# Sums of squares gathered with the residual, centring and scaling in turns, and two interleaved weight slots in a decoder trunk's LayerNorms

## The chip, the cores and the metric

The kernel runs on one core of one Trainium2 chip. The metric is the device time of one execution in microseconds (us), a median over several executions. The core's engines are TensorE (PE: matmuls; PEld is its weight load), VectorE (DVE), ScalarE (ACT), GpSimd (POOL) and SyncE (SP, which here only issues DMAs). Each engine works through its own list of instructions in order and waits on semaphores for the others.

## The reference

Two layers of a decoder trunk are computed for 512 prompt tokens and 8 x 4 sample tokens, 544 columns in all, with a model width of 1024. Each layer has a token mixer (RG-LRU, then gated DeltaNet), a cross-attention into 256 memory tokens, and a channel mixer (dense SwiGLU, then eight experts of which each token takes two). Each of these six sub-layers ends in a post-norm:

```python
def _layer_norm(x, g, b):
    mu = jnp.mean(xf, axis=-1, keepdims=True)
    var = jnp.mean(jnp.square(xf - mu), axis=-1, keepdims=True)
    return ((xf - mu) * lax.rsqrt(var + LN_EPS) * g + b).astype(x.dtype)

x = _layer_norm(DN_ALPHA * x + mix, p['ln_g'][i, 0], p['ln_b'][i, 0])
xa = _mem_attention(x, mem_k[i], mem_v[i], p['xa_wq'][i], p['xa_wo'][i])
x = _layer_norm(DN_ALPHA * x + xa, p['ln_g'][i, 1], p['ln_b'][i, 1])
ff = _swiglu(x, ...) if i % 2 == 0 else _moe_ffn(x, ...)
x = _layer_norm(DN_ALPHA * x + ff, p['ln_g'][i, 2], p['ln_b'][i, 2])
```

## The kernel before

The activations lie feature by feature: `x` has 128 partitions and 8 tiles (`KT`) of 544 columns. A mean over the features is therefore a matmul with a matrix of ones, which leaves the sum in all partitions. The columns are handled in two halves of 272, one PSUM bank each; `pair(i)` is banks 2i and 2i + 1.

**Weights.** A weight slot is a 1024 x 128 block of 512 KB. SP loads the slots in one fixed order into four buffers (`raw`). For the precise projections POOL splits each slot into a high part `wh` and a low part `wl`, of which there are two buffers each; the split of slot s + 2 waits until PE has used slot s (`w_used`). The activations are split too: `xh` and `xl`, or `hh` and `hl`. `lin_tile` then multiplies three groups of 16 matmuls, `wh` by `xh`, `wl` by `xh`, `wh` by `xl`, and signals `w_used` after the last. `linear` runs eight slots on alternating PSUM pairs. Keys and values of the memory (`kv`) take the raw slots as they are.

**The norms.** LN0 and LN1 follow the first layer's mixer and attention, LN2 its SwiGLU, LN3 and LN4 the second layer's mixer and attention. `layer_norm(5)` stands only in a branch for experts that overflow; the usual branch ends in another form of norm. Around a norm the engines do this:

- DVE, `residual`: for each tile that PE finishes, the new `x` (line 1666) and the running sum of the tiles (`add_tile`, L1656). In the SwiGLU (`experts`) the eight running sums come behind the last tile.
- PE, `layer_norm`: the ones-matmul of the sum (L570) into pair 2; then for LN0 to LN2 a part of the second layer's keys and values as filler (`KV1_AT` says which tiles: 4, 8 and 4 in the three norms; L600 for keys, L604 for values); then the ones-matmuls of the eight squares (L577) into pair 3; then the rest of the filler.
- DVE: eight centrings (L1644), and after the scale is known eight scalings (L1647), and eight low parts (L1633).
- ACT: eight squares (L1172) in two alternating buffers `lnsq`, then logarithm and exponential (L1177, L1178) for the inverse root, eight high parts (L1182), eight results (L1186). The copies of the filler's results (L1141 to L1145) stand between the squares and between the results. PE's next projection waits for the last of them (`kv_ev`).

The order is written by hand on each engine. Behind LN0 ACT sends half of the new keys to memory and waits for all outputs so far, since the next copies reuse that buffer:

```python
piece(0, 0)
act.wait_ge(w_used, S_LOUT + 8)
piece(0, 1)
piece(0, 2)
layer_norm(0)
act.dma_start(O["mem_k"][1][:, 0:4, :], A_st).then_inc(out_done, 16)
act.wait_ge(out_done, 80)
attention(0)
```

`piece` loads 2 MB of cached keys and values; it and the outputs of ACT go through ACT's own DMA queue. `attention` begins on PE with the query projection, on ACT with the copies of its eight tiles, one per slot; from its third slot on PE waits for such a copy (`q_ev`). Behind LN2 comes the DeltaNet's projection, which is interleaved with a side projection of `x` itself (L810); behind LN4 comes the router (L1022), which also reads `x`.

## Time and profile before

| | |
|---|---|
| Median of 3 runs | 2652.28 us (2652.21 to 2659.44) |
| The profiled execution's own time | 2667.02 us |
| Its span, first to last instruction | 2665.0 us |
| Mean granted TensorE clock | 0.931 of full speed |
| PE busy | 2407.8 us, 90% of the span |
| DVE busy | 854.4 us, 32% |
| ACT busy | 536.4 us, 20% |
| POOL busy | 961.3 us, 36% |
| Chain of waits: share of PE | 73% |
| Chain of waits: DVE, ACT, POOL | 10%, 3%, 2% |

The first rows say who works, the last two who sets the end: the chain is followed back from the last instruction, at each step to what released it. A timeline row has the start in us from the span's start, the duration in us, engine, line, operation, the tiles written and read, the count, and in brackets the idle time ahead of it with the engine and line that ended it. Rows with a count are several instructions merged.

### The profile page before, as it was taken

What the parts mean: (1) busy time and instruction counts of PE and PEld (TensorE: products, weight loads), DVE (VectorE), ACT (ScalarE), POOL (GpSimd) and SP (SyncE); (2) the same over time, 40 slices, a digit from 0 to 9 for tenths busy, and PEclk for the clock granted to TensorE, in tenths of its full rate; (3) what the DMA queues carried; (4) which work ended last, traced back from release to release, by engine and by line L of the source; (5) the groups of instructions that cost most, each with busy time, mean ns of one, the idle gap of its engine ahead of it and who ended that gap; (6) DMA issues with size and microseconds to landing.
All of it is one profiled execution on the core that took longest, in us unless ns stands there. A gap on an engine that the chain in (4) does not pass through costs nothing.

```text
span 2665.0 us, 42930 instructions
## 1 busy us (share of the span) xinstructions
PE 2407.8 (90%) x17290; PEld 2284.6 (86%) x17290; DVE 854.4 (32%) x1423; ACT 536.4 (20%) x1017; POOL 961.3 (36%) x1397
## 2 busy tenths in 40 slices
PE   8998889999999987999999888889689999999993
PEld 8988858899999967899989777777579999999993
DVE  3673222211011037666666542412301000000004
ACT  2450320310011033333322211321200000100103
POOL 4546614588888725433322103544100000000001
PEclk9999999999999988999988777899789999999996
DMA  7314341322222221211111101341255677788884
GB/s 285 99 61 177 126 182 59 115 88 79 88 87 87 79 71 59 58 59 59 58 52 59 35 25 64 148 160 64 79 188 180 220 238 238 232 266 268 279 286 161
DMA packets 98376, 347.55 MB, mean 130 GB/s; under 512 B 13488, under 2 KB 18736, under 8 KB 93344
## 3 DMA queue, kind: packets, MB, share of 16 engines
q1 hardware_dynamic: 73136, 279.08, 31.2%
q10 hardware_dynamic: 19056, 44.65, 4.7%
q0 software_dynamic: 6016, 21.43, 2.2%
q8 instruction: 122, 2.00, 0.3%
q14 instruction: 46, 0.38, 0.0%
HBM read 318.66 MB, written 26.47 MB: 130 GB/s over the span
## 4 chain that ended last, share of the span: by engine, by line
PE 73%; DVE 10%; issue 7%; DMA 4%; ACT 3%; POOL 2%; ACTq 0%; DVEq 0%; SPq 0%; POOLq 0%
PE ps L548 29%; PE ps L1073 14%; PE ps L1088 8%; PE ps L727 6%; DMA raw<-weights 2%; PE ps L600 2%; PE ps L577 2%; PE ps L604 1%; PE ps L936 1%; PE ps L638 1%; PE ps L932 1%; DVE x L1647 1%; PE ps L915 1%; POOL wl L471 1%; PE ps L774 1%
## 5 line engine op out<-in xcount | busy, mean ns | idle before, releaser
L467 POOL TENSOR_TENSOR wh<-raw,tab 128x256 fp32r<-128x256 f32 x672 | 425.5, 664 | 940.7 <-PE ps L548 744.2
L471 POOL TENSOR_TENSOR wl<-raw,wh 128x256 fp32r<-128x256 f32 x672 | 507.3, 785 | 0.0
L1073 PE MATMUL ps<-work,raw 128*128 128x128 f32 (+6 forms) x3072 | 424.8, 300 | 13.4 <-DMA raw<-weights 11.0
L1073 PEld LDWEIGHTS ps<-work,raw 128*128 128x128 f32 x3072 | 420.5, 191 | 16.3 <-DVE work L2112 6.8
L548 PE MATMUL ps<-xh,wh 128*128 128x272 f32 x2048 | 309.8, 304 | 41.4 <-ACT work L1353 10.6
L548 PEld LDWEIGHTS ps<-xh,wh 128*128 128x128 f32 x2048 | 282.4, 199 | 50.8 <-issue 18.2
L548 PE MATMUL ps<-xh,wl 128*128 128x272 f32 x2048 | 296.8, 295 | 0.0
L548 PE MATMUL ps<-xl,wh 128*128 128x272 f32 x2048 | 281.8, 288 | 1.5 <-DVE xl L1633 1.4
L548 PEld LDWEIGHTS ps<-xh,wl 128*128 128x128 f32 x2048 | 275.3, 193 | 1.8 <-issue 0.5
L548 PEld LDWEIGHTS ps<-xl,wh 128*128 128x128 f32 x2048 | 265.5, 188 | 2.6 <-DVE xl L1633 2.6
L517 POOL DMA_DIRECT2D rows_y<-moe_h x8 | 4.3, 538 | 656.9 <-DVE moe_h L2105 656.9
L1088 PE MATMUL ps<-work,raw 128*128 128x128 f32 (+6 forms) x1536 | 218.0, 298 | 0.8 <-DVE work L2112 0.8
L1088 PEld LDWEIGHTS ps<-work,raw 128*128 128x128 f32 x1536 | 209.6, 190 | 1.6 <-DVE work L2112 1.4
L2112 DVE TENSOR_TENSOR work<-moe_h,ps 128x128 f32<-128x128 f32 (+6 forms) x96 | 30.6, 319 | 440.1 <-ACT moe_h L1563 440.1
L1563 ACT ACTIVATE moe_h<-ps 128x128 f32<-128x128 f32 (+6 forms) x96 | 29.0, 302 | 396.4 <-PE ps L1073 396.3
L1713 DVE TENSOR_TENSOR work<-work,ps 128x544 f32<-128x544 f32 x24 | 17.3, 721 | 225.8 <-PE ps L548 225.8
L2105 DVE COPY moe_h<-ps 128x256 f32<-128x256 f32 (+1 forms) x64 | 25.1, 391 | 197.2 <-PE ps L1061 155.6
L727 PE MATMUL ps<-hh,wh 128*128 128x272 f32 x384 | 81.4, 294 | 6.7 <-DVE hl L1633 6.7
L727 PE MATMUL ps<-hh,wl 128*128 128x272 f32 x384 | 80.4, 292 | 0.0
L727 PE MATMUL ps<-hl,wh 128*128 128x272 f32 x384 | 80.4, 292 | 0.0
L1172 ACT ACTIVATE lnsq<-x 128x544 f32<-128x544 f32 x40 | 26.3, 657 | 210.0 <-DVE x L1644 195.0
L1666 DVE SCALAR_TENSOR_TENSOR x<-x,ps 128x544 f32<-128x544 f32 x32 | 23.1, 721 | 139.9 <-PE ps L548 139.9
(358 smaller groups left out, 3121.3 us busy)
## 6 DMA issues: line engine op xcount, KB each, us to landing
raw<-weights SPq DMA_DIRECT2D x488, 512.0 KB, 3.9
moe_h<-cache SPq DMA_DIRECT2D x6, 2048.0 KB, 8.9
moe_h<-cache ACTq DMA_DIRECT2D x4, 2048.0 KB, 13.6
work<-cache SPq DMA_DIRECT2D x4, 2048.0 KB, 8.9
moe_h<-rows_x POOLq DMA_DIRECT2D x14, 512.0 KB, 7.8
rows_x<-lnsq ACTq DMA_DIRECT2D x9, 512.0 KB, 11.0
work<-scratch ACTq DMA_DIRECT2D x16, 272.0 KB, 4.2
work<-cache ACTq DMA_DIRECT2D x2, 2048.0 KB, 10.4
```

The lines of the kernel that those rows point to most:

```text
L467: nc.gpsimd.tensor_tensor(flat(h1[:, k0:k1]), flat(r1[:, k0:k1]), one_col, MUL).then_inc(pool_hi, 1)
L471: low = nc.gpsimd.tensor_tensor(flat(l1[:, k0:k1]), flat(r1[:, k0:k1]), flat(h1[:, k0:k1]).bitcast(F), SUB)
L548: last = mm(ps[:, 2 * i + h, 0:HT], w[:, par_, k, :], a[:, k, h * HT:(h + 1) * HT], start=(n == 0 and k == 0), stop=(n == 2 and k == KT - 1))
L577: last = mm(ps[:, 6 + h, 0:HT], ones, lnsq[:, k % 2, h * HT:(h + 1) * HT], start=(k == 0), stop=(k == KT - 1))
L600: last = mm(ps[:, b, 0:MEM], raw[:, q, k, :], A_mem[:, k, :], start=(k == 0), stop=(k == KT - 1))
L604: last = mm(ps[:, b, mt * P:(mt + 1) * P], A_mem[:, k, mt * P:(mt + 1) * P], raw[:, q, k, :], start=(k == 0), stop=(k == KT - 1))
L638: last = mm(ps[:, 4 + tt // 2, (tt % 2) * MEM:(tt % 2 + 1) * MEM], A_q[:, 2 * h + kk, tt * P:(tt + 1) * P], A_k[:, 2 * h + kk, :], start=( ...
L727: last = mm(ps[:, 2 * d + h, 0:HT], w[:, s % 2, k, :], a[:, f, h * HT:(h + 1) * HT], start=(f == 0 and m == 0), stop=(f == FT - 1 and m == 2))
L1073: last = mm(ps[:, j // 2, (j % 2) * c:(j % 2 + 1) * c], raw[:, slot % RAW, k, :], M_x[:, r % 2, k, 0:c], start=(k == 0), stop=(k == KT - 1))
L1088: last = mm(ps[:, 2 + d % 2, 0:c], raw[:, slot % RAW, k, :], M_h[:, f, 0:c], start=(f == 0), stop=(f == FT - 1))
L1563: s(A(M_s[:, f % 2, 0:c], ps[:, f % 2, 0:c], ACT.Silu), m_silu, e12 + f + 1)
L2112: s(V.tensor_tensor(M_h[:, f, 0:c], M_s[:, f % 2, 0:c], ps[:, f % 2, c:2 * c], MUL), m_h, e12 + f + 1)
```

## The change

The sums of squares are now formed ahead of the norm, from tiles that are not yet centred. While the last projection runs, ACT squares each new tile (`squares`) and DVE adds it (`add_square`, after `add_tile`). PE then makes two ones-sums, of the tiles and of the squares. ACT squares the mean, DVE subtracts it from the mean of squares, and clamps at zero. The centring, which needs the mean alone, moves behind: DVE centres tile 0 and tile 1 while it waits, then centres and scales by turns. The ones-sums swap their PSUM pairs. In the SwiGLU the running sums move to the tiles of the second half, whose loop is written out.

The filler is cut otherwise: one tile stands ahead of the ones-sums, all others behind; their copies on ACT stand between the high parts. Behind LN0, LN1 and LN3 the first two slots of the next projection are interleaved: both groups with `xh` of slot 0 and slot 1, then both groups with `xl`. ACT issues the cache pieces of LN0 and LN3 behind the norm. In the router's loop the first turns move from k = 3 to k = 5 and wait for LN4's last scaling. The norm of the overflow branch keeps the old form as `last_norm`.

```diff
-KV1_AT = {0: (0, 2, 4), 1: (4, 7, 12), 2: (12, 14, 16)}
+KV1_AT = {0: (0, 4), 1: (4, 12), 2: (12, 16)}
...
             def linear(slot, direct, ah, al, freed, base, fresh=None):
-                for s in range(8):
+                if fresh is not None:
+                    pairs = [lin_steps(slot + s, direct, s, s, ah, al, fresh=fresh, per=2 * KT) for s in range(2)]
+                    for steps in pairs:
+                        next(steps)
+                        next(steps)
+                    for steps in pairs:
+                        for _ in steps:
+                            pass
+                for s in range(0 if fresh is None else 2, 8):
...
             def layer_norm(n):
+                if n in KV1_AT:
+                    lo, hi = KV1_AT[n]
...
+                    kv(1, lo, lo + 1)
+                pe.wait_ge(z_sum, n + 1)
+                for h in range(2):
+                    last = mm(ps[:, 6 + h, 0:HT], ones, lnsq[:, 0, h * HT:(h + 1) * HT], start=True, stop=True)
+                last.then_inc(ln_sum, 1)
+                pe.wait_ge(z_sq, n + 1)
+                for h in range(2):
+                    last = mm(ps[:, 4 + h, 0:HT], ones, lnsq[:, 1, h * HT:(h + 1) * HT], start=True, stop=True)
+                last.then_inc(ln_var, 1)
+                if n in KV1_AT:
+                    kv(1, lo + 1, hi)
+                    pe.wait_ge(kv_ev, 16 + hi)
...
+            def squares(n):
+                act.preload_act_table_set("natural_log_exp_and_others")
+                for t in range(KT):
...
+                    if t >= 2:
+                        act.wait_ge(z_acc, (KT - 2) * n + t - 1)
+                    s(A(lnr[:, :] if t else lnsq[:, 1, :], x[:, t, :], ACT.Square), z_pw, KT * n + t + 1)
...
             def layer_norm(n):
...
+                act.wait_ge(ln_sum, n + 1)
+                s(A(two(lnsq[:, 0, :]), pair(3), ACT.Square, scale=D ** -0.5), z_mean, n + 1)
+                if lo < hi:
+                    kv(1, lo)
+                act.wait_ge(z_var, n + 1)
+                s(A(lnr[:, :], lnr[:, :], ACT.Ln, bias=pc("eps5"), scale=1.0 / D))
+                s(A(lnr[:, :], lnr[:, :], ACT.Exp, scale=-0.5), ln_std, n + 1)
...
+                for k in range(KT):
+                    upper(n, k)
+                    if lo + 1 + k < hi:
+                        kv(1, lo + 1 + k)
+                for k in range(KT):
+                    result(n, k)
...
             piece(0, 0)
+            squares(0)
+            layer_norm(0)
             act.wait_ge(w_used, S_LOUT + 8)
             piece(0, 1)
             piece(0, 2)
-            layer_norm(0)
             act.dma_start(O["mem_k"][1][:, 0:4, :], A_st).then_inc(out_done, 16)
...
             def layer_norm(n):
+                dve.wait_ge(z_mean, n + 1)
+                centre(0)
+                dve.wait_ge(ln_var, n + 1)
+                s(V.tensor_tensor(two(lnr[:, :]), pair(2), two(lnsq[:, 0, :]), SUB))
+                s(V.tensor_scalar(lnr[:, :], lnr[:, :], 0.0, None, ALU.max), z_var, n + 1)
+                centre(1)
+                dve.wait_ge(ln_std, n + 1)
+                for k in range(KT):
+                    if k >= 2:
+                        centre(k)
+                    s(V.tensor_tensor(x[:, k, :], x[:, k, :], lnr[:, :], MUL), ln_n, n * KT + k + 1)
...
+            def add_square(t, n):
+                if t:
+                    dve.wait_ge(z_pw, KT * n + t + 1)
+                    add = V.tensor_tensor(lnsq[:, 1, :], lnsq[:, 1, :], lnr[:, :], ADD)
```

The order of the instructions shows it at three places. On ACT, around LN0, from the first cache piece (`work<-cache`, `moe_h<-cache` are the pieces) to the query copies at the end, the list before was:

```order
L1199 DMA work<-cache 128x2x2048
L1199 DMA moe_h<-cache 128x2x2048 x2
L1167 ACT_TABLE_LOAD
L1172 ACTIVATE lnsq<-x 128x544
L1141 ACTIVATE work<-ps 128x256
...
L1182 ACTIVATE xh<-x,par 128x544 x8
...
L1186 ACTIVATE x<-x,par 128x544 x6
L1329 DMA out_mem_k<-work 128x1024
L1204 ACTIVATE work<-ps 128x544 x8
```

The squares, the filler's copies and the results followed the pieces. On ACT at the same place it is now:

```order
L1265 DMA work<-cache 128x2x2048
L1202 ACT_TABLE_LOAD
L1210 ACTIVATE lnsq<-x 128x544
L1210 ACTIVATE lnr<-x 128x544 x7
L1225 ACTIVATE lnsq<-ps 128x544
...
L1214 ACTIVATE xh<-x,par 128x544 x5
L1219 ACTIVATE x<-x,par 128x544 x8
L1265 DMA moe_h<-cache 128x2x2048 x2
L1396 DMA out_mem_k<-work 128x1024
L1270 ACTIVATE work<-ps 128x544 x8
```

Two of the three pieces moved from ahead of the norm to a place directly ahead of the key output. On PE, around LN1, from the last group of the output projection to the first slots of the SwiGLU, the list before was:

```order
L548 MATMUL ps<-xl,wh 128x272 x16
L570 MATMUL ps<-lnsq,tab 128x272 x2
L600 MATMUL ps<-work,raw 128x256 x24
L577 MATMUL ps<-lnsq,tab 128x272 x16
L600 MATMUL ps<-work,raw 128x256 x8
L604 MATMUL ps<-raw,work 128x128 x64
L548 MATMUL ps<-xh,wh 128x272 x16
L548 MATMUL ps<-xh,wl 128x272 x16
L548 MATMUL ps<-xl,wh 128x272 x16
```

PE now has at this place:

```order
L548 MATMUL ps<-xl,wh 128x272 x16
L624 MATMUL ps<-work,raw 128x256 x8
L586 MATMUL ps<-lnsq,tab 128x272 x2
L590 MATMUL ps<-lnsq,tab 128x272 x2
L624 MATMUL ps<-work,raw 128x256 x24
L628 MATMUL ps<-raw,work 128x128 x64
L548 MATMUL ps<-xh,wh 128x272 x16
L548 MATMUL ps<-xh,wl 128x272 x16
L548 MATMUL ps<-xh,wh 128x272 x16
L548 MATMUL ps<-xh,wl 128x272 x16
L548 MATMUL ps<-xl,wh 128x272 x32
```

Sixteen ones-matmuls became two, one filler tile moved ahead of them, and the two groups with `xl` of slots 0 and 1 moved behind all four groups with `xh`. On DVE, the last tile ahead of LN1 and the norm, before:

```order
L1666 SCALAR_TENSOR_TENSOR x<-x,ps 128x544
L1656 TENSOR_TENSOR lnsq<-lnsq,x 128x544
L1644 SCALAR_TENSOR_TENSOR x<-ps,x 128x544 x8
L1647 TENSOR_TENSOR x<-x,lnr 128x544 x8
L1633 TENSOR_TENSOR xl<-x,xh 128x544 x8
```

DVE now has there, down to the second turn of centring and scaling:

```order
L1762 SCALAR_TENSOR_TENSOR x<-x,ps 128x544
L1745 TENSOR_TENSOR lnsq<-lnsq,x 128x544
L1752 TENSOR_TENSOR lnsq<-lnsq,lnr 128x544
L1714 SCALAR_TENSOR_TENSOR x<-ps,x 128x544
L1719 TENSOR_TENSOR lnr<-ps,lnsq 128x544
L1720 TENSOR_SCALAR lnr<-lnr 128x544
L1714 SCALAR_TENSOR_TENSOR x<-ps,x 128x544
L1726 TENSOR_TENSOR x<-x,lnr 128x544 x2
L1714 SCALAR_TENSOR_TENSOR x<-ps,x 128x544
L1726 TENSOR_TENSOR x<-x,lnr 128x544
```

The sum of squares joined each tile of the projection, and six of the eight centrings moved between the scalings.

## Rows read from the trace of the kernel before

**Rows 1.** Timeline of PE around LN0 (columns as described above).

```profile
261.33 1.19 PE L570 MATMUL ps<-lnsq,tab 128*128 128x272 f32 x4 [1.64 <-DVE lnsq L1656]
...
269.26 8.03 PE L577 MATMUL ps<-lnsq,tab 128*128 128x272 f32 x32
...
291.21 4.00 PE L548 MATMUL ps<-xh,wh 128*128 128x272 f32 x16 [7.01 <-ACT work L1141]
...
305.36 2.16 PE L548 MATMUL ps<-xh,wh 128*128 128x272 f32 x16
```

**Rows 2.** Timelines of DVE (scalings of LN1, then LN0) and ACT (high parts, LN1).

```profile
477.46 6.04 DVE L1647 TENSOR_TENSOR x<-x,lnr 128x544 f32<-128x544 f32 x8 [13.87 <-ACT lnr L1178]
...
278.89 8.75 DVE L1647 TENSOR_TENSOR x<-x,lnr 128x544 f32<-128x544 f32 x8 [10.24 <-ACT lnr L1178]
...
478.29 6.96 ACT L1182 ACTIVATE xh<-x,par 128x544 fp32r<-128x544 f32 x8 [0.93 <-DVE x L1647]
```

**Rows 3.** Timeline of PE around LN1.

```profile
452.46 2.16 PE L548 MATMUL ps<-xl,wh 128*128 128x272 f32 x16
...
512.13 2.18 PE L548 MATMUL ps<-xh,wh 128*128 128x272 f32 x16
```

**Rows 4.** Timelines of DVE and PE around LN2.

```profile
946.23 0.72 DVE L1722 SCALAR_TENSOR_TENSOR x<-x,ps 128x544 f32<-128x544 f32 x1 [5.25 <-PE ps L727]
...
947.92 4.51 DVE L1656 TENSOR_TENSOR lnsq<-lnsq,x 128x544 f32<-128x544 f32 x6
...
971.18 7.31 PE L604 MATMUL ps<-raw,work 128*128 128x128 f32 x64
...
990.27 7.51 PE L810 MATMUL ps<-x,par 128*8 128x272 f32 x64
```

**Rows 5.** Timeline of PE around LN3.

```profile
1683.33 2.16 PE L548 MATMUL ps<-hl,wh 128*128 128x272 f32 x16
...
1724.34 2.18 PE L548 MATMUL ps<-xh,wh 128*128 128x272 f32 x16
```

**Rows 6.** Timeline of PE around LN4; L1022 is the router, here four tiles.

```profile
1872.19 2.16 PE L548 MATMUL ps<-xl,wh 128*128 128x272 f32 x16
...
1890.20 8.12 PE L1022 MATMUL ps<-par,x 128*128 128x8 f32 x40 [3.31 <-ACT x L1186]
```

**Rows 7.** Timeline of POOL: halves of splits in several stretches.

```profile
299.67 2.33 POOL L467 TENSOR_TENSOR wh<-raw,tab 128x256 fp32r<-128x256 f32 x4 [12.61 <-PE ps L548]
301.95 2.81 POOL L471 TENSOR_TENSOR wl<-raw,wh 128x256 fp32r<-128x256 f32 x4
...
418.48 2.81 POOL L467 TENSOR_TENSOR wh<-raw,tab 128x256 fp32r<-128x256 f32 x4 [0.89 <-PE ps L548]
...
430.60 2.81 POOL L467 TENSOR_TENSOR wh<-raw,tab 128x256 fp32r<-128x256 f32 x4 [0.54 <-PE ps L548]
...
1647.89 3.29 POOL L467 TENSOR_TENSOR wh<-raw,tab 128x256 fp32r<-128x256 f32 x4 [0.40 <-PE ps L548]
...
1660.49 3.29 POOL L467 TENSOR_TENSOR wh<-raw,tab 128x256 fp32r<-128x256 f32 x4 [0.46 <-PE ps L548]
...
278.63 3.78 POOL L467 TENSOR_TENSOR wh<-raw,tab 128x256 fp32r<-128x256 f32 x4
282.37 4.70 POOL L471 TENSOR_TENSOR wl<-raw,wh 128x256 fp32r<-128x256 f32 x4
```

**Rows 8.** DMA issues: out<-in, queue, count, size each, median us to landing.

```profile
out_mem_k<-work ACTq DMA_DIRECT2D x1, 512.0 KB, 2.7
...
out_gdn_conv<-work ACTq DMA_DIRECT2D x8, 40.5 KB, 1.6
...
out_lru_h<-work ACTq DMA_DIRECT2D x1, 36.0 KB, 6.0
```

**Rows 9.** Stretches: length, busy us by engine (count), PEclk, DMA share, GB/s.

```profile
268.00:270.00 2.00, 2.00 (x11) 1.73 (x10) 0.66 (x1) 0.38 (x1) 0.00 (x0) 1.00 1.00 424
...
292.00:296.00 4.00, 4.00 (x21) 4.00 (x20) 3.27 (x5) 3.83 (x6) 0.00 (x0) 0.53 0.01 2
```

More of the change, by code:

```diff
@@ L697, in up @@
                     def up(g):
-                        for j in range(4):
+                        opening = isinstance(g, int) and isinstance(e, int) and e == 0
+                        if opening:
+                            ge(pe, f_h, e12 - 1)
+                            pairs = [lin_steps(e36 + j, direct, j, j, xh, xl, fresh=KT * (first_ln - 1), per=2 * KT)
+                                     for j in range(2)]
+                            for steps in pairs:
+                                next(steps)
+                                next(steps)
+                            for steps in pairs:
+                                for _ in steps:
+                                    pass
+                        for j in range(2 if opening else 0, 4):
                             if j % 2 == 0:
                                 ge(pe, f_h, e12 + g * 2 + (j // 2 - 1))
-                            lin_tile(e36 + g * 4 + j, direct, j % 2, j, xh, xl,
-                                     fresh=KT * (first_ln - 1) if j == 0 and isinstance(g, int) and isinstance(e, int) else None)
+                            lin_tile(e36 + g * 4 + j, direct, j % 2, j, xh, xl)
                     ge(pe, f_y, e8)
@@ L1025, in _ @@
                     last.then_inc(r_pe, 1)
-                if k == 3:
+                if k == 5:
+                    pe.wait_ge(ln_n, KT * 4 + KT)
                     turn_tokens(0, EARLY)
@@ new lines, in upper, with result @@
+            def upper(n, k):
+                act.wait_ge(ln_n, n * KT + k + 1)
+                s(A(xh[:, k, :], x[:, k, :], ACT.Identity, bias=pc("lnb", n * 8 + k, n * 8 + k + 1),
+                    scale=pc("lng", n * 8 + k, n * 8 + k + 1)), ln_xh, n * KT + k + 1)
+            def result(n, k):
+                act.wait_ge(ln_n, n * KT + k + 1)
+                s(A(x[:, k, :], x[:, k, :], ACT.Identity, bias=pc("lnb", n * 8 + k, n * 8 + k + 1),
+                    scale=pc("lng", n * 8 + k, n * 8 + k + 1)), ln_x, n * KT + k + 1)
@@ L1175, in layer_norm @@
[L1175 removed]
+                        act.wait_ge(ln_var, n + k - 1)
+                    s(A(lnsq[:, k % 2, :], x[:, k, :], ACT.Square), ln_sq, k + 1)
+                act.wait_ge(ln_var, n + KT)
                 s(A(two(lnr[:, :]), pair(3), ACT.Ln, bias=pc("eps5"), scale=1.0 / D))
                 s(A(lnr[:, :], lnr[:, :], ACT.Exp, scale=-0.5), ln_std, n + 1)
[L1179 to L1183 removed]
@@ L1184, in layer_norm @@
-                for k in range(KT):
-                    act.wait_ge(ln_n, n * KT + k + 1)
-                    s(A(x[:, k, :], x[:, k, :], ACT.Identity, bias=pc("lnb", n * 8 + k, n * 8 + k + 1),
-                        scale=pc("lng", n * 8 + k, n * 8 + k + 1)), ln_x, n * KT + k + 1)
-                    if k < hi - mid:
-                        kv(1, mid + k)
-                    if n == NLN - 1 and k >= KT - NT:
+                for k in range(KT):
+                    result(n, k)
+                    if k >= KT - NT:
@@ L1331, in _ @@
             attention(0)
+            squares(1)
             layer_norm(1)
@@ L1337, in _ @@
             experts(HALVES, S_FFN, 0, False)
+            squares(2)
             layer_norm(2)
@@ L1521, in _ @@
             act.dma_start(A_v, O["mem_v"][1]).then_inc(mem_in, 16)
+            squares(3)
+            layer_norm(3)
             act.wait_ge(w_used, S_GOUT + 8)
@@ L1529, in _ @@
             s(A(M_tri, tc("mincl"), ACT.Exp), r_act, TRIANGLE)
+            squares(4)
             layer_norm(4)
@@ L1723, in one @@
                           f_y, e8 + (d + 1))
-                repeat(dve, n, one, s)
-                for k in range(KT):
-                    add_tile(k, n_ln)
+                        if isinstance(e, int) and e + 1 == n:
+                            add_tile(d, n_ln)
+                            add_square(d, n_ln)
+                if gated:
+                    repeat(dve, n, one, s)
+                else:
+                    for e in range(n):
+                        one(e)
             def log1p_half(e, t0, t1, t2):
```

63 lines of the change are left out of this document (34 added, 29 removed).

## Prediction

> **What bounds the kernel now.** The share of each engine on the page says that TensorE (PE) is the resource, and the chain of waits confirms it; the change touches the stretches where PE stands aside. I looked for these in the PE timeline around each of the first five LayerNorms, then in the DVE, ACT and POOL timelines of the same stretches for what PE waits for, and in the list of DMA issues for what is queued. A stretch runs from E, the end of the last matmul ahead of a norm, to the start of the third weight slot of the next projection (by then the one-off waits are over), or to the end of the side projection L810 in LN2, or to the start of the router in LN4. The lengths are
>
> - LN0: E is 261.33 - 1.64 = 259.69, third slot 305.36: 45.7 us [rows 1]
> - LN1: E is 452.46 + 2.16 = 454.6, third slot 512.13: 57.5 us [rows 3]
> - LN2: E about 946.1 (the residual starts 0.1 behind it), L810 ends at 990.27 + 7.51 = 997.8: 51.7 us [rows 4]
> - LN3: 1683.33 + 2.16 = 1685.5 to 1724.34: 38.85 us [rows 5]
> - LN4: 1872.19 + 2.16 = 1874.35 to 1890.20: 15.85 us [rows 6]
>
> In each, the squares run as a chain after the centring: centre on DVE, square on ACT, ones-matmul on PE, eight times; PE's 32 ones-matmul passes take 8.0 us [rows 1] and fillers stand in front of them.
>
> **The new head.** Passes cost: DVE 6.04/8 = 0.755 us, ACT 6.96/8 = 0.87 us [rows 2], a ones-sum (two matmuls, four passes) 1.2 us [rows 1]. After E come residual and running sum (1.6 us), the ones-sum, the mean's square on ACT (0.87), centre, subtraction and clamp on DVE (2.3), then Ln and Exp (1.5 to 1.75): the first scaling starts at about E + 7.5. The sum of squares costs one DVE pass of 0.755 after the running sum and is ready at E + 2.4; its ones-sum hides under the mean's square. Where a filler stands in front (LN0 to LN2; one takes 7.31/2 = 3.65 us [rows 4]) the head ends at E + 9.3. Against that, centring is no longer done ahead: 14 passes on DVE follow (8 scalings, 6 centrings), 10.6 us, so the last scaling ends at E + 18.0, or 19.9 with filler. Where POOL splits weights at the same time a scaling takes 8.75/8 = 1.09 instead of 0.755 [rows 2]; for some seven scalings that is 2.4 more (LN0, LN2).
>
> **LN1.** PE is the limit: filler 3.65, both ones-sums 2.0, seven fillers 25.5, copy 0.5: the projection starts at E + 31.7, with seven high parts ready and the eighth due at once. The two interleaved slots hold 12 us of matmuls and hide the low parts (ready at E + 40). But slot 0 now frees its buffer only at E + 41.7, and the POOL split of slot 2 waits for that: 2.33 + 2.81 = 5.14 [rows 7] and 0.4 for hand-overs, E + 47.2. PE stands still 3.5 us. After a standstill of 7.01 us the first 16 matmuls took 4.00 instead of 2.16 us [rows 1], at a granted clock of 0.53, 1.2 instead of 2.4 GHz [rows 9]; I charge 2.0 for such a start. 57.5 - 49.2 = **8.3 gained**.
>
> **LN2.** The seven running sums behind the last residual (4.51 for six [rows 4]) move under the down-projection. The last high part is at E + 9.3 + 10.6 + 2.4 + 0.9 = 23.2; 14 more matmuls, with a slow start, end at E + 27.3 and L810 needs 7.5: E + 34.8. 51.7 - 34.8 = **16.9 gained** (18.9 without the slow start). DVE and ACT behind L810 keep their order, so the whole delta-rule stage shifts along.
>
> **LN3.** No fillers. Last high part E + 19.0; the other three groups of 16 with a slow start, E + 27.3 (low parts at 26.8 are hidden); slot 0 finished at 29.3, split 34.8, slow start 36.8. 38.85 - 36.8 = **2.0 gained**. ACT issues the three cache loads behind the norm, but their first reader is a whole projection away.
>
> **LN4.** First result at 7.5 + 0.75 + 0.87 = E + 9.1; the router needs about 2 us per tile [rows 6] and results come every 1.5, so PE runs through: **6.7 gained**. Moving the turns to k = 5 changes no count; their new wait for the last scaling (E + 18) is over by then.
>
> **At nothing.** The table load of ACT moves ahead of the first residual, and the eight squares into the projection, where ACT has no other work in the order; were it late, the last square would stand in for the running sum beside it and cost at most its 0.87. The unrolled halves on DVE issue the same passes. The norm of the other branch keeps its old form and is not on the path.
>
> **LN0, where the change pays.** ACT issues two cache pieces ahead of the norm today; after the change they stand behind all eight results, and directly behind them on the same queue stands the 512 KB output of memory keys. ACT waits for that output before it copies the first query, and PE's third slot waits for the copy. Today that output lands in 2.7 us [rows 8], since nothing is in front of it. A 36 KB output (of the first mixer, issued right behind 2 MB of keys and values) took 6.0 us on this queue, a 40.5 KB one with nothing ahead 1.6 [rows 8]: the queue hands over in order. The results end at E + 23.2 + 7.0 = 30.2. Then 4.7 MB at the 424 GB/s of a saturated stretch [rows 9] take 11.1; with one weight tile between (1.2) and 1.5 to start, the output lands at E + 44, the copy ends at 44.7, slow start 46.7: **1.0 lost** against 45.7. The bound on the other side is a landing in 2.7: then only the split counts, E + 37 + 2 = 39, 6.7 gained. I take the loss, since the 6.0 us row is the same queue in the same situation. The Trainium skill, "DMA: Bandwidth & Descriptors", Queues, rings and completion order, says that each DMA engine takes one queue's descriptors in ring order, though completion is not strictly first-in-first-out. By its order alone the sum is mine; the row of 6.0 us agrees with it.
>
> **The price in the projections ahead of the norms.** The added sum is a DVE pass with both inputs in SBUF. POOL feels these: its first half of a split takes 2.33 without, 2.81 with one, 3.29 with two such passes per tile [rows 7], 0.48 each. With one, two slots take 430.60 - 418.48 = 12.12 us; with two, 1660.49 - 1647.89 = 12.60 [rows 7]: in LN3, which has two already, PE follows POOL. The added pass therefore costs 0.48 per two slots. Slots 3, 5 and 7 form the chain: 1.44 us in LN0, LN1 and LN4. In LN3 the third pass makes POOL 6.55 per slot, serially: 1.8. In LN2's down stage both passes are new: about 1.5 (bounds 0.5 and 2). Sum 7.6. The squares on ACT lie beside PE's 6 us per tile.
>
> [...]
>
> **Sum.** -1.0 + 8.3 + 16.9 + 2.0 + 6.7 = 32.9; minus 7.6 = 25.3 us. The profiled execution took 2667.0 us (its span 2665.0), the median of three is 2652.3, 0.55% less; the differences are tens of microseconds, so I take 25 off the median too: **2627 us**.
>
> **Rivals.**
> - A, the output overtakes the pieces in LN0: 7.7 better, 2619. For it: two queues share the engines freely. Against: the 6.0 us row.
> - B, each added pass stops POOL for its full 0.755: a slot with two takes 6.65 instead of 6.1, and the five projections lose about 20 instead of 7.6: 2639. Against: 0.48 per pass in two places.
> - C, the change doesn't do what it says: the squares come late (ACT waits for DMAs ahead of LN3), or the time saved goes into a later wait (the expert weights of the last third arrive by DMA): about 2649. Against: every later load is released by a semaphore behind the norms, so it shifts along.
> - D, slower: POOL becomes the bound of all five projections. Under a run of back-to-back DVE passes a slot took 3.78 + 4.70 = 8.48 us [rows 7]. If three passes per tile brought that, some 25 slots would lose 2.4 each, 60 instead of 7.6: 2679. It decides for a loss over 0.3% from about 7.4 us per slot. Against: DVE has 2.3 to 3.0 us of work in 6 (three or four passes).
>
> **How the numbers follow.** Forecast 0.62, A 0.17, B 0.13, C 0.05, D 0.03. A measurement of this kernel can tell 0.3%, 8 us, from no change. Forecast, A and B all lie beyond that: faster 0.91, same 0.06, slower 0.03. Range: the terms' own bounds (LN2 13 to 19, LN1 6 to 9, slow starts 0 to 3 each) make it 10 wide on either side of the forecast, A and B stretch it to 2606 and 2642.
>
> **What would show it.** The rows of after: third slot of LN1 about 47 us behind E, the end of L810 about 35, the router's start about 9; POOL's two-slot pitch 12.6 in the projections ahead of LN0, LN1 and LN4; in LN0 the first query copy at about E + 44 and the key output with 12 or more us to landing. If that output lands early, or if POOL's pitch stays 12.1, the gain is larger; if the pitch is 13.3, smaller. I am wrong if the two interleaved slots don't wait for POOL, or if a stage behind the norms does not shift along.

## The result, and the profile after

| | before | after |
|---|---|---|
| Median, 18 runs each | 2662.24 us (2651.43 to 2669.37) | 2643.80 us (2638.74 to 2649.45) |
| Ratio, 95% interval | | 0.9936 [0.9924, 0.9947] |
| The profiled execution, own time (span) | 2667.02 (2665.0) | 2640.61 (2638.8) |

The change makes the kernel 18.4 us faster. The forecast was 2627 with a range from 2606 to 2642; 2643.8 lies just above that range. The two profiled executions differ by 26.4 us, the forecast says 25.3, the medians differ by 18.4. Two questions follow: do the terms of the sum hold, and why do the traces show more than the medians?

The page of after, busy time by engine:

```profile
PE 2371.2 (90%) x17150; PEld 2255.9 (85%) x17150; DVE 896.0 (34%) x1468; ACT 539.9 (20%) x1022; POOL 979.2 (37%) x1397
```

DVE has 42 us more (854.4 before); the 35 added sums are 33.4 of them. POOL has 18 us more (961.3) although it does the same work; 35 times the 0.48 us of a pass is 16.8. PE has 37 us less.

Timeline of PE after the change, at the stretches of [rows 1, 3, 4, 5, 6]; L624 and L628 are filler, L586 the first ones-sum, L844 the side projection, L1056 the router:

```profile
256.15 2.16 PE L548 MATMUL ps<-hl,wh 128*128 128x272 f32 x16
...
304.29 4.00 PE L548 MATMUL ps<-xh,wh 128*128 128x272 f32 x16 [11.46 <-ACT work L1270]
...
456.96 2.18 PE L548 MATMUL ps<-xl,wh 128*128 128x272 f32 x16
...
489.85 2.24 PE L548 MATMUL ps<-xh,wh 128*128 128x272 f32 x16 [0.78 <-ACT moe_h L1180]
...
505.83 3.24 PE L548 MATMUL ps<-xh,wh 128*128 128x272 f32 x16 [3.74 <-POOL wl L471]
...
941.95 0.41 PE L761 MATMUL ps<-hh,wl 128*128 128x272 f32 x2
...
946.92 1.08 PE L586 MATMUL ps<-lnsq,tab 128*128 128x272 f32 x4
...
969.99 7.98 PE L844 MATMUL ps<-x,par 128*8 128x272 f32 x64
...
1666.91 2.16 PE L548 MATMUL ps<-hl,wh 128*128 128x272 f32 x16
...
1705.20 3.62 PE L548 MATMUL ps<-xh,wh 128*128 128x272 f32 x16 [3.27 <-POOL wl L471]
...
1856.68 2.17 PE L548 MATMUL ps<-xl,wh 128*128 128x272 f32 x16
...
1867.81 12.15 PE L1056 MATMUL ps<-par,x 128*128 128x8 f32 x60 [5.22 <-ACT x L1219]
```

From E (start plus duration of the first row of each pair) the third slot of LN1 is at 505.83 - 459.14 = 46.7 us (57.5 before), the end of L844 at 977.97 - 942.36 = 35.6 (51.7), the router at 1867.81 - 1858.85 = 9.0 (15.85). In LN1 and LN3 PE stands still for 3.74 and 3.27 us ahead of the third slot and takes 3.24 and 3.62 us for its first 16 matmuls instead of 2.16; the granted clock in these two rows is 0.65 and 0.57 of 2.4 GHz, so for a good part of them it is at the lower of its two levels, 1.2 GHz.

The queue behind LN0: ACT's rows, and the DMA issue of the key output (size, us to landing), which [rows 8] had at 2.7:

```profile
287.73 0.92 ACTq L1265 DMA_DIRECT2D moe_h<-cache  x2
288.68 0.49 ACTq L1396 DMA_DIRECT2D out_mem_k<-work  x1
303.62 1.28 ACT L1270 ACTIVATE work<-ps 128x544 f32<-128x544 f32 x2 [15.92 <-DMA out_mem_k<-work]
...
out_mem_k<-work ACTq DMA_DIRECT2D x1, 512.0 KB, 14.9
```

Timeline of POOL ahead of LN0: the first half of a split takes 3.29 with two sums of DVE beside it, the running sum and the added one, and the pitch of two slots is 245.86 - 233.26 = 12.60 us, where [rows 7] had 12.12 with one pass; PE's wait at the next slot:

```profile
233.26 3.29 POOL L467 TENSOR_TENSOR wh<-raw,tab 128x256 fp32r<-128x256 f32 x4 [0.50 <-PE ps L548]
...
245.86 3.29 POOL L467 TENSOR_TENSOR wh<-raw,tab 128x256 fp32r<-128x256 f32 x4 [0.50 <-PE ps L548]
...
239.48 2.24 PE L548 MATMUL ps<-hh,wh 128*128 128x272 f32 x16 [0.33 <-POOL wl L471]
```

### The profile page after: what moved, and what is told of

It is laid out like the page before. It is cut to its first block, busy times and chain, and to the rows that moved or that the text cites. A ratio compares the mean times of both kernels' runs of the same rounds, so it can differ in the third digit from the quotient of the medians.

```text
span 2638.8 us, 42746 instructions
## 1 busy us (share of the span) xinstructions
PE 2371.2 (90%) x17150; PEld 2255.9 (85%) x17150; DVE 896.0 (34%) x1468; ACT 539.9 (20%) x1022; POOL 979.2 (37%) x1397
## 4 chain that ended last, share of the span: by engine, by line
PE 63%; issue 16%; DVE 9%; POOL 6%; DMA 4%; ACT 2%; ACTq 0%; POOLq 0%; DVEq 0%; SPq 0%
PE ps L548 24%; PE ps L1108 14%; PE ps L1123 8%; PE ps L761 4%; POOL wl L471 3%; DMA raw<-weights 2%; POOL wh L467 2%; PE ps L624 2%; PE ps L628 1%; PE ps L970 1%; PE ps L966 1%; PE ps L949 1%; PE ps L808 1%; DVE x L1726 1%; PE ps L915 1%
## 5 line engine op out<-in xcount | busy, mean ns | idle before, releaser
L467 POOL TENSOR_TENSOR wh<-raw,tab 128x256 fp32r<-128x256 f32 x672 | 438.8, 683 | 907.5 <-PE ps L548 744.0
L761 PEld LDWEIGHTS ps<-hh,wh 128*128 128x128 f32 x384 | 61.5, 193 | 8.7 <-issue 8.2
L1210 ACT ACTIVATE lnr<-x 128x544 f32<-128x544 f32 x35 | 23.1, 660 | 212.4 <-DVE x L1762 155.4
## 6 DMA issues: line engine op xcount, KB each, us to landing
rows_x<-lnsq ACTq DMA_DIRECT2D x9, 512.0 KB, 10.8
```

Source lines behind the costliest of these rows:

```text
L467: nc.gpsimd.tensor_tensor(flat(h1[:, k0:k1]), flat(r1[:, k0:k1]), one_col, MUL).then_inc(pool_hi, 1)
L761: last = mm(ps[:, 2 * d + h, 0:HT], w[:, s % 2, k, :], a[:, f, h * HT:(h + 1) * HT], start=(f == 0 and m == 0), stop=(f == FT - 1 and m == 2))
```

## The experiments

Each kernel is timed beside the kernel before on the same chip, whose median there was 2660.2 to 2663.4 us; ratios are to that median.

**Both kernels once more.** after_again is the changed kernel, before_again (one execution) the one before.

> The changed kernel once more, to see what differs between two executions of one program. My theory: the stretches that the change touches repeat within 0.5 us each (third slot of LN1 at E + 46.7, end of the side projection in LN2 at E + 35.6, router at E + 9.0), and the spread of some 10 us in the whole time comes from other stretches: the attention, the DeltaNet's heads and the experts, where the same matmuls fall under a lowered clock at one time and not at another. So the point by point list up to the last LayerNorm gives again about 20 us against the kernel before, and the whole time 2644, 17 to 19 under it. Rival: the terms themselves scatter, and the 26 us of the first pair of traces do not return in the stretches.

> The kernel before once more, for a second trace of it. My theory: the stretches at the norms repeat (LN1 57.5 us, LN3 38.85, LN4 15.85), while the experts (642.5 us in the first trace) and the down-projections of the SwiGLU differ by some us with the granted clock and the waits for weights, as they do among the traces of the changed kernels (638.9 to 646.8 us). Its whole time lies between 2651 and 2669. Rival: the stretches at the norms are what scatters.

Measured: after_again 2640.31 us, ratio 0.9924 [0.9910, 0.9937]; before_again 2663.61. Lengths of all stretches, worked out from the starts and ends of PE's rows in the four traces. A norm runs here to the start of the fourth slot, so that its slow start is inside; a projection is counted from its second slot on:

| stretch, us | before | again | after | again | mean change | forecast |
|---|---|---|---|---|---|---|
| projection ahead of LN0 | 42.54 | 42.54 | 43.96 | 43.96 | +1.4 | +1.4 |
| LN0, E to fourth slot | 51.67 | 51.82 | 54.13 | 54.13 | +2.4 | +1.0 |
| first attention | 100.87 | 101.16 | 102.81 | 102.64 | +1.7 | 0 |
| projection ahead of LN1 | 42.39 | 42.50 | 43.88 | 43.91 | +1.5 | +1.4 |
| LN1, E to fourth slot | 63.54 | 63.42 | 54.33 | 54.34 | -9.1 | -8.3 |
| SwiGLU up to the last down stage | 354.46 | 353.88 | 352.54 | 352.56 | -1.6 | 0 |
| last down stage | 73.49 | 73.51 | 76.36 | 74.97 | +2.2 | +1.5 |
| LN2, E to end of side projection | 51.65 | 51.69 | 35.61 | 34.84 | -16.4 | -16.9 |
| DeltaNet's heads | 643.87 | 640.51 | 645.80 | 644.91 | +3.2 | 0 |
| projection ahead of LN3 | 43.84 | 43.86 | 45.30 | 45.29 | +1.5 | +1.8 |
| LN3, E to fourth slot | 44.89 | 44.93 | 43.59 | 43.55 | -1.3 | -2.0 |
| second attention | 101.52 | 101.73 | 102.31 | 102.23 | +0.7 | 0 |
| projection ahead of LN4 | 42.45 | 42.49 | 43.88 | 43.90 | +1.4 | +1.4 |
| LN4, E to router | 15.85 | 15.85 | 8.96 | 8.95 | -6.9 | -6.7 |
| experts | 642.47 | 644.50 | 638.91 | 642.61 | -2.7 | 0 |
| start, router, tail | 349.44 | 346.67 | 346.42 | 347.04 | -1.3 | 0 |

The stretches at the norms repeat within 0.2 us, except the down stage and LN2 of after (1.4 and 0.8). The stretches with a forecast sum to -23.5 us (forecast -25.3). The first attention, the SwiGLU, the heads and the second attention add +3.9 and make it -19.6; the experts and the start take it to the -23.7 by which the traces differ. These last two scatter: over all traces of both kernels and the variants below the experts take 636.1 to 646.8 us. So about -19.6 is to be expected in medians, and they give -18.4 and -19.9. That the first pair of traces differs by 26.4, close to the forecast, is luck: its experts and its start happen to give 6.6 of it.

In the down stage both traces of after have the same three waits of PE for POOL (0.22, 0.30 and 0.37 us), which before has not. The 1.4 us between them are the clock: the first 7 us of the stage in after, and in after_again (length, then busy us of PE, PEld, DVE, ACT, POOL with counts, PEclk, DMA share, GB/s):

```profile
866.00:873.00 7.00, 7.00 (x34) 7.00 (x35) 0.00 (x0) 0.00 (x0) 2.17 (x4) 0.57 0.25 77
```

```profile
866.84:873.84 7.00, 7.00 (x45) 7.00 (x46) 0.00 (x0) 0.00 (x0) 2.16 (x4) 0.79 0.25 77
```

At the clock of after_again the stage loses the 1.5 us that were forecast; both lengths occur among the variants below.

Four stretches were forecast at nothing. How much of them PE is busy, and how much it is not:

| stretch, us | PE busy before, again | after, again | not busy before, again | after, again |
|---|---|---|---|---|
| first attention | 87.3, 87.3 | 89.2, 89.1 | 13.6, 13.8 | 13.6, 13.6 |
| SwiGLU up to the last down stage | 346.4, 345.9 | 344.5, 344.5 | 8.0, 8.0 | 8.0, 8.0 |
| DeltaNet's heads | 570.1, 564.6 | 568.1, 567.4 | 73.7, 76.0 | 77.7, 77.5 |
| second attention | 87.8, 87.6 | 87.5, 87.6 | 13.8, 14.1 | 14.8, 14.7 |

Why the same matmuls take longer in the first attention: the stretch before, and after (columns as above):

```profile
342.00:404.60 62.60, 49.48 (x388) 30.34 (x389) 17.44 (x21) 20.46 (x47) 4.77 (x8) 0.97 0.48 185
```

```profile
343.00:409.00 66.00, 52.77 (x388) 32.85 (x388) 17.36 (x21) 20.69 (x47) 5.06 (x8) 0.92 0.45 175
```

Here 388 matmuls take 49.5 us at a granted clock of 0.97 and 52.8 at 0.92. The list of waits has nothing new. The lower of the clock's two levels (1.2 of 2.4 GHz) falls on other matmuls. In after, the first slot behind this stretch gives 1.5 us back (6.1 instead of 7.6), and the SwiGLU in both traces 1.6 us; from 640 to 700 us the granted clock is 0.94 in before and 0.97 in after. What moves it is not shown; of the traces of the variants below only output_first's has the first attention as short as before (101.4).

In the second attention PE is no busier than before. What grows is one wait of PE for a cache piece (total, times, longest; before, then after; 0.9 and 1.5 in the second traces):

```profile
PE ps L630 <- DMA moe_h<-cache: 0.5, 1, 0.5
```

```profile
PE ps L654 <- DMA moe_h<-cache: 1.6, 1, 1.6
```

In the variants, which issue these pieces in the same order, it lies between nothing and 1.6, so the later issue need not be the cause.

In the heads, too, PE is no busier after; it waits 2.8 us longer in the mean. PE's own time there differs most between the two traces of before (the stretch ahead of the projection of LN3; before, then before_again):

```profile
1470.00:1634.20 164.20, 127.69 (x680) 114.84 (x678) 74.16 (x126) 33.16 (x59) 8.98 (x12) 0.70 0.08 28
```

```profile
1469.00:1628.40 159.40, 122.59 (x676) 109.84 (x676) 73.69 (x126) 33.15 (x59) 8.48 (x11) 0.72 0.09 29
```

PE is 5 us less busy with the same instructions (some records are missing in each), at 0.72 instead of 0.70. So a part of the heads' 3.2 us is scatter between the two traces of before. All twelve traces of the changed kernel and its variants lie between 644.2 and 645.8, above both of before (643.9 and 640.5): some cost is there, its size and cause are open.

**output_first: what the queue behind LN0 costs.**

```diff
+act.dma_start(O["mem_k"][1][:, 0:4, :], A_st).then_inc(out_done, 16)
 act.wait_ge(w_used, S_LOUT + 8)
 piece(0, 1)
 piece(0, 2)
-act.dma_start(O["mem_k"][1][:, 0:4, :], A_st).then_inc(out_done, 16)
```

> Only the order of three DMA issues behind LN0 is changed: key output first, then the two cache pieces. My theory: the queue hands over in order, so the output lands 2.7 us behind its issue instead of 14.9, the copy of the first query follows slot 0 at once, and the third slot starts when POOL has split it (295.9 in the trace of after) instead of at 304.29: about 8 us faster than the changed kernel, 2636. Rival: the output shares the engines with SP's transfers and lands late whatever stands in front of it on its own queue: less than 3 us.

Measured: 2633.11 us, ratio 0.9894 [0.9878, 0.9909], 7.2 under after_again. Its third slot of LN0, and the key output:

```profile
298.45 3.60 PE L548 MATMUL ps<-xh,wh 128*128 128x272 f32 x16 [3.34 <-POOL wl L471]
...
out_mem_k<-work ACTq DMA_DIRECT2D x1, 512.0 KB, 3.6
```

The landing falls from 14.9 to 3.6 us, PE now waits for the split alone, and LN0 up to the fourth slot takes 46.3 instead of 54.1 us. The order within one queue decides. Compared with the kernel before (51.7), the norm itself gains 5.4 us in LN0; the moved pieces had eaten it.

**no_pair: the two interleaved slots.**

```diff
-                for s in range(0 if fresh is None else 2, 8):
+                for s in range(8):
...
-                    lin_tile(slot + s, direct, s % 2, s % 2, ah, al)
+                    lin_tile(slot + s, direct, s % 2, s % 2, ah, al, fresh=fresh if s == 0 else None)
...
-                            for steps in pairs:
-                                next(steps)
-                                next(steps)
                             for steps in pairs:
```

The last part is the start of the SwiGLU, the projection behind LN1.

> Only the interleaving of the first two slots behind LN0, LN1 and LN3 is undone: slot 0 whole, then slot 1. What the interleaving is for: without it PE stands still until the low parts come, so this is slower by some us. My theory from the trace: in LN1 the low parts come one each 0.85 us from 491.41 on, while PE begins at 489.85, so slot 0 ends at about 498.6 instead of 500.1, POOL can split the third slot 1.5 us earlier, and slot 1 fills the time until then, so that neither the wait of 3.7 us nor the slow start behind it remains: third slot at about 504.6 at full clock instead of 505.83 with 1.6 more behind: 2.8 us faster there; in LN3 by the same reasoning 3.6 us (slot 0 ends at 1697 instead of 1700); LN0 unchanged, where the output is waited for. Together some 5 us faster than the changed kernel, 2638.

Measured: 2633.48 us, ratio 0.9899 [0.9882, 0.9917], 6.8 under after_again. Timeline of PE in LN1, from the last `xl` pieces of slot 0 to the third slot:

```profile
499.74 0.52 PE L548 MATMUL ps<-xl,wh 128*128 128x272 f32 x2 [0.35 <-DVE xl L1693]
500.10 2.17 PE L548 MATMUL ps<-xh,wh 128*128 128x272 f32 x16
...
506.11 2.16 PE L548 MATMUL ps<-xh,wh 128*128 128x272 f32 x16
```

PE now waits 0.2 to 0.4 us for each low part, but slot 0 ends earlier, and slot 1 covers the split of slot 2: no standstill at the third slot, no slow start. LN1 takes 51.55 instead of 54.33 us up to the fourth slot, LN3 39.86 instead of 43.57: 2.8 and 3.7, as expected. The interleaving hides the low parts and makes POOL wait for it.

**squares_psum and sums_psum: what POOL feels.**

squares_psum changes the add of the squares (and lets ACT write them to `pair(2)`), sums_psum also the running sum, of which only the last add writes SBUF; LN2 stays as it is, since its down-projection uses all PSUM banks:

```diff
-                    add = V.tensor_tensor(lnsq[:, 1, :], lnsq[:, 1, :], lnr[:, :], ADD)
+                    if n == 2:
+                        add = V.tensor_tensor(lnsq[:, 1, :], lnsq[:, 1, :], lnr[:, :], ADD)
+                    else:
+                        add = V.tensor_tensor(two(lnsq[:, 1, :]), two(lnsq[:, 1, :]), pair(2), ADD)
...
-                if t:
+                if t and n in (2, 5):
                     s(V.tensor_tensor(lnsq[:, 0, :], x[:, 0, :] if t == 1 else lnsq[:, 0, :], x[:, t, :], ADD),
...
+                elif t:
+                    s(V.tensor_tensor(two(lnsq[:, 0, :]) if t == KT - 1 else pair(3), two(x[:, 0, :]) if t == 1 else pair(3),
+                                      two(x[:, t, :]), ADD),
```

> In the four projections ahead of LN0, LN1, LN3 and LN4, ACT writes the squares of tiles 1 to 7 to PSUM (the free pair 2) instead of SBUF, so that the added DVE pass has one input in SBUF and one in PSUM. My theory: what POOL feels is a DVE pass with both inputs in SBUF; then the added pass costs POOL nothing, its two-slot pitch returns from 12.60 to 12.12 us, PE's waits of 0.3 us at slots 3, 5 and 7 fall to under 0.05, and about 1.4 us return in each of the four projections: 5.8 us faster than the changed kernel, 2638. Rival: any DVE pass that writes SBUF holds POOL up, and the pitch stays at 12.60: no gain.

> Besides the squares, the running sums of the same four projections are kept in PSUM (pair 3; the last add writes SBUF). My theory, by which POOL feels only DVE passes with both inputs in SBUF: hardly any such pass is left, POOL's half splits fall to 2.33 us and its pitch under 12.0 for two slots, so PE sets the pace in LN0, LN1 and LN4 and the rest of about 0.1 us per two slots goes; ahead of LN3 one such pass per tile is left (x is put together from high and low part), 6.1 us per slot as in the other projections before. Against the kernel with the squares alone some 1 us more, against the changed kernel 5 to 6 us in these stretches, 2636 in all. Rival: the writes count too, and the pitch stays above 12.0.

Measured: squares_psum 2638.31 us, ratio 0.9919 [0.9905, 0.9933], 2.0 under after_again; sums_psum 2631.09, ratio 0.9894 [0.9876, 0.9912]. POOL ahead of LN0, first squares_psum (two slots apart), then sums_psum (one slot apart):

```profile
235.84 2.81 POOL L467 TENSOR_TENSOR wh<-raw,tab 128x256 fp32r<-128x256 f32 x4 [0.54 <-PE ps L548]
...
247.97 2.81 POOL L467 TENSOR_TENSOR wh<-raw,tab 128x256 fp32r<-128x256 f32 x4 [0.54 <-PE ps L548]
```

```profile
239.69 2.33 POOL L467 TENSOR_TENSOR wh<-raw,tab 128x256 fp32r<-128x256 f32 x4 [0.88 <-PE ps L548]
...
245.69 2.33 POOL L467 TENSOR_TENSOR wh<-raw,tab 128x256 fp32r<-128x256 f32 x4 [0.88 <-PE ps L548]
```

The same DVE passes run; each that takes one operand from PSUM gives POOL 0.48 us back: 3.29, 2.81, 2.33, and a two-slot pitch of 12.60, 12.13, 12.00. DVE gains as well: its pass of the added sum, in after and in squares_psum,

```profile
235.06 1.02 DVE L1752 TENSOR_TENSOR lnsq<-lnsq,lnr 128x544 f32<-128x544 f32 x1
```

```profile
237.64 0.72 DVE L1756 TENSOR_TENSOR lnsq<-lnsq,ps 128x544 f32<-128x544 f32 x1
```

takes 1.02 us beside POOL's split with both operands in SBUF, and 0.72 with one in PSUM; after POOL's last split ahead of LN0 it takes 0.73 in after too. Each holds up the other: POOL loses 0.48, DVE 0.30. The four projections lose their whole price with the squares alone (-5.6 us) and 1.3 more with the sums. The Trainium skill, "SBUF — State Buffer", Who interferes with whom, says that a DVE instruction with at most one SBUF input (outside its two-port modes) doesn't contend with GpSimd, and these rows agree. Of the 5.6 us (5.8 expected) only 2.0 show in squares_psum's median; in its trace the slow start in LN1 is 1.0 us longer, and in LN3, where the third slot comes 0.8 earlier, 1.3. sums_psum gained more than the 5 to 6 us that I expected: 0.3% of the kernel before, 8 us, by the two ratios.

**sum_behind and centre_first: two parts of the change undone.**

In sum_behind LN2's running sums stand behind the last tile, in centre_first all centrings ahead of the first scaling:

```diff
                         if isinstance(e, int) and e + 1 == n:
+                            add_square(d, n_ln)
+                    if isinstance(e, int) and e + 1 == n:
+                        for d in range(KT):
                             add_tile(d, n_ln)
-                            add_square(d, n_ln)
```

```diff
-                centre(1)
+                for k in range(1, KT):
+                    centre(k)
                 dve.wait_ge(ln_std, n + 1)
                 for k in range(KT):
-                    if k >= 2:
-                        centre(k)
```

> One part undone: in LN2 the running sums stand behind the last tile again; the sums of squares stay under the down-projection. My theory: the mean is known some 4.5 us later (six adds of 0.75 us, which PE waits for, since only one filler tile stands in front), so the stretch from E to the end of the side projection grows from about 35.2 to 39.7; the down stage ahead of it gives back 0.7 to 1.4 us of POOL's price. Net 3 to 4 us slower than the changed kernel, 2645. Rival: the moved sums cost POOL as much as they save behind it, then no change.

> One part undone: all eight centrings stand ahead of the first scaling, instead of in turns with it. My theory: the last scaling comes at the same time as before (E + 18), so that LN0 to LN3, which wait for the last high part or for fillers, stay within 0.5 us; only LN4, where the router follows the results tile by tile, starts later: six centrings of 0.755 minus what fitted into the wait for the scale, 3 to 4.5 us. So 4 us slower than the changed kernel, 2645. Rival: every norm loses these 4 us, 20 in all.

Measured: sum_behind 2639.73 us, ratio 0.9921 [0.9906, 0.9937], the same as after_again: the rival held. The down stage falls from 75.0 or 76.4 to 73.6 us, LN2 grows from 34.8 or 35.6 to 36.9. PE's first ones-sum in sum_behind:

```profile
947.44 1.99 PE L586 MATMUL ps<-lnsq,tab 128*128 128x272 f32 x4 [3.04 <-DVE lnsq L1745]
```

It waits 3.04 us, at E + 7.8; in after it follows its filler without a wait, at E + 4.6. My 4.5 us missed two things. The filler hides a part of the adds, so the head is only 3.2 us later. And PE makes up more behind it: its first two groups take 6.7 us instead of 9.9 (9.6 in after_again), since it waits 1.4 instead of 2.6 us for high parts and runs at full clock (1.00 in the second group, 0.50 in after). So moving the running sums under the down-projection brought nothing. What is left for the gain in LN2 is the squares and the order of the fillers, which no run separates.

centre_first 2651.16 us, ratio 0.9962 [0.9951, 0.9974], 10.8 over after_again. LN4 loses the 3.7 us that I expected (8.96 to 12.66). What I had left out is LN1, which loses 3.7 as well. There ACT copies each filler's result behind a high part, and high parts now start later, so a filler waits for its bank:

```profile
475.04 3.72 PE L624 MATMUL ps<-work,raw 128*128 128x256 f32 x16 [2.43 <-ACT moe_h L1178]
```

LN0 loses 1.0, LN2 about 1, LN3 gains 1.4; the rest lies in the attention and in scatter. So centring in turns is worth 7 (against 2643.8) to 11 us, more than LN4 alone.

**all_three, fillers_behind, copies_spread: towards a better kernel.** all_three puts output_first, no_pair and sums_psum together; all_three_again is the same kernel beside the next one.

> Key output ahead of the two pieces, no interleaving, squares and running sums in PSUM, all three. My theory: the gains add, and in LN0 the first two meet: with the output out of the way the third slot is bound by the split, and without the interleaving slot 0 is free 2 us earlier, so PE runs from slot 1 into slot 2 without a standstill and without a slow start, 2 to 3 us more. 7 + 7 + 3 + 2 = some 19 us under the changed kernel, 2622. Rival: the three overlap (each merely moves the same wait), then no better than the best of them, 2633.

Measured: 2618.64 us, ratio 0.9843 [0.9827, 0.9858]; again 2620.80, 0.9845 [0.9827, 0.9863]. The gains add: 0.81% of the kernel before under after_again, and 0.85% for the three apart. LN0 takes 42.6 us up to the fourth slot (54.1 after, 46.3 with output_first alone), since neither the output nor the split is late any more; PE's third slot of LN0 in all_three follows the second without a wait and at full pace:

```profile
291.90 2.16 PE L548 MATMUL ps<-xl,wh 128*128 128x272 f32 x16
293.90 2.16 PE L548 MATMUL ps<-xh,wh 128*128 128x272 f32 x16
```

fillers_behind is all_three with all filler tiles of LN0 and LN2 behind the ones-sums on PE (and the first of their copies behind the exponential on ACT); copies_spread, on top of it, moves the other copies on ACT behind the high parts 3, 5 and 7:

```diff
...
-                    kv(1, lo + 1, hi)
+                    kv(1, lo + 1 if n == 1 else lo, hi)
...
```

```diff
-                    if lo + 1 + k < hi:
+                    if n == 1 and lo + 1 + k < hi:
                         kv(1, lo + 1 + k)
+                    elif n in (0, 2) and k in (2, 4, 6):
+                        kv(1, lo + k // 2)
```

> The combination, with one more part of the change undone: in LN0 and LN2 no filler tile stands ahead of the ones-sums (in LN1 it stays, since PE is the limit there). My theory from the trace of the combination: in LN0 the ones-sums start at 260.59, while the sum is ready at 258.9; in LN2 at 932.04, while it is ready at 929.1. Without the tile in front the whole head moves forward by 1.7 and 2.9 us, and the tile finds room behind, where PE waits for high parts anyway (0.4 to 1.3 us per tile): 4.6 us faster than the combination, 2614. Rival: PE stands still at the head instead, its clock falls, and the tile takes its 3.65 us later: no gain or 2 us slower.

> The kernel with the fillers behind the ones-sums, and ACT's copies of the filler's results in LN0 and LN2 stand behind the third, fifth and seventh high part instead of behind the first three. My theory from the trace of that kernel: in LN0 nothing was gained, because ACT, which works in order, stood at these copies for 1.8 to 2.2 us each, waiting for PE's fillers, while scaled tiles were ready (the last scaling ended at 276.1, the last high part at 279.7). With the copies later the last high part comes at 277, and the results, the low parts and the second slot 2.7 us earlier in LN0, about 2.4 in LN2: 5 us faster than with the fillers behind alone, 2610. Rival: PE's last fillers now wait for their banks, which these copies free, and the gain is lost there: no change.

Measured: fillers_behind 2615.51 us, ratio 0.9827 [0.9810, 0.9843], 5.3 under all_three_again; copies_spread **2608.77 us** (2605.85 to 2619.03), ratio 0.9814 [0.9790, 0.9838]. In fillers_behind LN2 gained 2.8 us, LN0 nothing: ACT stood at the copies; the rest of the 5.3 lies in no norm. ACT's rows in LN0, between the exponential and the last high parts:

```profile
267.58 0.84 ACT L1202 ACTIVATE xh<-x,par 128x544 fp32r<-128x544 f32 x1 [0.56 <-DVE x L1718]
268.45 0.38 ACT L1163 ACTIVATE work<-ps 128x256 f32<-128x256 f32 x1
...
276.16 0.85 ACT L1202 ACTIVATE xh<-x,par 128x544 fp32r<-128x544 f32 x1 [0.48 <-DVE x L1718]
```

Those are of copies_spread: no copy between the high parts waits, and the last high part ends at 277.0; in fillers_behind it is this:

```profile
274.92 0.38 ACT L1163 ACTIVATE work<-ps 128x256 f32<-128x256 f32 x1 [2.19 <-PE ps L614]
275.34 4.34 ACT L1202 ACTIVATE xh<-x,par 128x544 fp32r<-128x544 f32 x5
```

Five high parts queue behind a copy that waits 2.19 us. With the copies later, LN2 gains 2.5 us more; in LN0 the second slot starts 1.7 earlier, of which a slow start takes back 1.3. The trace shows this step; the medians don't settle it, since the two intervals overlap. copies_spread beats both kernels: 32 us under after_again, 35 under after, 1.9% under before.

## Why the prediction was wrong, and where it was right

- **What bounds, and the new head**: right. Every row named under "what would show it" came: LN1's third slot at 46.7 (47), the side projection at 35.6 and 34.8 (35), the router at 9.0 (9), POOL's pitch 12.60 (12.6), the first query copy at 303.62, E + 45.3 (44), the key output 14.9 us to landing (12 or more).
- **LN1**: right in mechanism, with PE's standstill of 3.7 us (3.5); 0.8 us better in the table. **LN2**: right in size, 16.4 (16.9); of its parts, the moved running sums are worth 1.3 to 2.0 us there, and the down stage takes that back (sum_behind). **LN3**: 1.3 instead of 2.0, since slot 0 freed its buffer at E + 30.9 instead of 29.3. **LN4**: right, 6.9 (6.7).
- **LN0**: right in mechanism, as output_first shows; under-sized by 1.4 us, because the third slot began at E + 46.0 instead of 44.7: the results ended as forecast (the output was issued at E + 30.4), but pieces and output took 14.9 us instead of 13.8. Rival A is out: the output did not overtake the pieces.
- **The price in the projections**: right, 0.48 us per pass: 1.4 to 1.5 in four projections; in the down stage 2.2 (1.5), of which 0.7 is the clock at its start. As a mechanism it was shown by squares_psum and sums_psum for the four projections. Rival B is out, and D too: POOL's slot ahead of LN3 takes 6.5 us. The 0.755 that B charges is a pass without POOL beside it; beside a split the pass takes 1.02 to 1.05, and the loss is shared, 0.48 for POOL and 0.30 for DVE. The Trainium skill ("SBUF — State Buffer", Who interferes with whom) says of DVE's two-port modes that the later of two instructions fully blocks; for a pass with two SBUF inputs it says that it contends, and gives no size.
- **At nothing**: here a cost was missed. No work changes in the attentions, the SwiGLU and the heads, but their times do. The lower clock falls on other matmuls: +1.7 us in the first attention, -1.6 in the SwiGLU. And PE waits longer: 0.7 in the second attention, where the prediction held the later cache loads to be harmless, and up to 3 in the heads. Together that takes 4 of the 25 us back. Rival C spoke of time that goes into later waits; these are such waits, but small, and not for late squares or the experts' weights.
- **The sum: the step that failed.** "I take 25 off the median too" set the difference against a median of three runs, 2652.28. Over 18 runs that median is 2662.24; two of the three lay at the low end of a spread of 18 us, and the profiled execution of 2667 stood beside them. This alone is 10 of the 16.8 us by which the forecast missed; 25.3 off 2662.24 gives 2636.9, inside the range. The other 6.9 us are the terms: 1.8 in the stretches counted, 3.9 in those taken as unchanged, and 1.2 that no stretch explains. The range took in the bounds of the terms and none for the base.
- **What stays open**: with two traces of the kernel before, how much of the heads' 3.2 us belongs to the change; and why the lower clock moves from the SwiGLU into the first attention.

## What to carry to other kernels

Judge a base by its spread: where one profiled execution lies above the highest of three timed runs, the range must take that in. A gain at a norm is soon limited by the next engine in order (POOL's split, a copy queued on ACT, an output behind loads on one queue), so look at what each in-order engine has ahead of the piece that is needed first. Interleaving that hides a late operand can release a buffer later; compare the two waits before choosing.

## What the runs showed of the hardware

- A DVE sum with both operands in SBUF and POOL's split beside it hold each other up: 0.48 us for POOL, and 1.02 to 1.05 us instead of 0.72 for the pass. With one operand in PSUM both losses are gone.
- A 512 KB output took 14.9 us behind 4 MB of loads on the same queue, and 3.6 ahead of them.
- A wait of 3.3 to 3.7 us ahead of a weight slot was followed by 16 matmuls of 3.2 to 3.6 us instead of 2.16 (granted clock 0.57 to 0.65), one of 11.5 us by 4.0 (0.50); waits of 0.2 to 0.4 us between pairs of matmuls, as in no_pair's LN1, were not (1.00).
- The experts, with the same instructions, took 636.1 to 646.8 us. Waits of PE for weights there (total, times, longest) in after, and in output_first:

```profile
PE ps L1108 <- DMA raw<-weights: 8.9, 9, 2.0
```

```profile
PE ps L1108 <- DMA raw<-weights: 14.1, 12, 3.0
```

These two take 638.9 and 646.8 us: 5 us of the difference are waits for the weights, 3 are PE's own time, 628.75 us busy in after and 631.99 in output_first.
